# Low parts of two weight halves made in one operation of 4096 columns, with the halves in paired slots

## The reference

```
def swiglu(h, w_gu, w_down):
    g, u = jnp.split(h @ w_gu, 2, axis=-1)
    return (jax.nn.silu(g) * u) @ w_down

def moe_swiglu(h, router_w, w_gu, w_down):
    ...
    for e in range(N_EXPERTS):      # 8 experts, w_gu[e] 1024 x 7168, w_down[e] 3584 x 1024
        out = out + cw[:, e:e + 1] * swiglu(xf, w_gu[e], w_down[e])
```

## Time and profile before

| | |
|---|---|
| median of 3 runs | 1671.43 us (1670.72 to 1672.18) |
| the profiled execution | 1670.79 us |
| its span, first to last instruction | 1669.0 us |
| TensorE busy | 1639.0 us (98%) |
| VectorE busy | 1319.3 us (79%) |
| ScalarE busy | 1102.0 us (66%) |
| read from memory | 484.94 MB, 292 GB/s over the span |

### The profile page before, as it was taken

One profiled execution on the slowest core, in us unless ns is written; L12 is line 12 of the kernel. 1 busy time (PEld: TensorE's weight loads), 2 busy tenths in 40 slices (PEclk: granted clock), 3 DMA queues, 4 the chain that ended last, 5 costly groups with the idle time before them and its releaser, 6 DMA issues.

```text
span 1669.0 us, 23179 instructions
## 1 busy us (share of the span) xinstructions
PE 1639.0 (98%) x8338; PEld 1373.9 (82%) x8338; DVE 1319.3 (79%) x1133; ACT 1102.0 (66%) x1076; POOL 225.6 (14%) x398
## 2 busy tenths in 40 slices
PE   9999999999999999999999999999999999999996
PEld 7988888888889888888888788887888887888875
DVE  6567656545465677468999999889999899998997
ACT  5355744444444557447768887778887688877885
POOL 0034440000000344407920000000000000000000
PEclk9999999999999999999999999999999999999998
DMA  8654544555545444536998999989999899999894
GB/s 339 264 177 152 187 179 164 202 184 193 179 173 177 169 159 171 188 147 254 412 379 348 417 421 401 409 334 397 421 398 418 348 374 419 419 399 379 341 422 199
DMA packets 71792, 488.74 MB, mean 293 GB/s; under 512 B 8651, under 2 KB 11932, under 8 KB 13212
## 3 DMA queue, kind: packets, MB, share of 16 engines
q1 hardware_dynamic: 69052, 483.89, 74.3%
q10 hardware_dynamic: 2656, 3.70, 0.7%
HBM read 484.94 MB, written 2.62 MB: 292 GB/s over the span
## 4 chain that ended last, share of the span: by engine, by line
PE 82%; DVE 9%; DMA 4%; issue 3%; ACT 1%; DVEq 0%; SPq 0%; ACTq 0%
PE bank L418 20%; PE bank L420 20%; PE bank L419 20%; DMA w_raw<-expert_slabs 3%; PE bank L1941 3%; PE bank L1942 3%; DVE w_lo L414 3%; PE bank L1722 3%; PE bank L1724 3%; PE bank L1725 3%; DVE e_v L411 2%; DVE e_uy L414 2%; PE bank L1920 2%; PE bank L1958 1%; DVE e_bias L414 1%
## 5 line engine op out<-in xcount | busy, mean ns | idle before, releaser
L414 DVE TENSOR_TENSOR w_lo<-w_raw,w_hi 128x2048 fp32r<-128x2048 f32 x288 | 654.5, 2292 | 210.2 <-ACT w_hi L405 209.8
L405 ACT ACTIVATE w_hi<-w_raw 128x2048 fp32r<-128x2048 f32 x288 | 551.2, 1918 | 389.3 <-PE bank L420 280.5
L418 PE MATMUL bank<-w_hi,hT 128*128 128x512 f32 x720 | 285.2, 396 | 1.9 <-DVE w_lo L1167 1.9
L420 PE MATMUL bank<-w_hi,hT 128*128 128x512 f32 x720 | 281.3, 391 | 0.0
L419 PE MATMUL bank<-w_lo,hT 128*128 128x512 f32 x720 | 280.8, 390 | 0.0
L418 PEld LDWEIGHTS bank<-w_hi,hT 128*128 128x128 f32 x720 | 135.5, 188 | 28.6 <-issue 2.1
L420 PEld LDWEIGHTS bank<-w_hi,hT 128*128 128x128 f32 x720 | 135.4, 188 | 28.7
L419 PEld LDWEIGHTS bank<-w_lo,hT 128*128 128x128 f32 x720 | 135.7, 188 | 26.8
L414 DVE TENSOR_TENSOR e_uy<-w_raw,e_k 128x2048 fp32r<-128x2048 f32 x56 | 128.2, 2288 | 16.7 <-ACT e_k L405 16.6
L411 DVE TENSOR_TENSOR e_v<-w_raw,hT 128x2048 fp32r<-128x2048 f32 x55 | 125.8, 2288 | 10.8 <-ACT hT L402 10.7
L405 ACT ACTIVATE e_k<-w_raw 128x2048 fp32r<-128x2048 f32 x56 | 107.5, 1920 | 34.3 <-PE bank L420 22.3
(11 more groups left out here) (355 smaller groups left out, 3125.9 us busy)
## 6 DMA issues: line engine op xcount, KB each, us to landing
w_raw<-expert_slabs SPq DMA_DIRECT2D x334, 1024.0 KB, 7.4
w_raw<-mix_slabs SPq DMA_DIRECT2D x88, 1024.0 KB, 4.8
w_raw<-dense_slabs SPq DMA_DIRECT2D x33, 1024.0 KB, 4.8
bias_lines<-bias ACTq DMA_DIRECT2D x1, 1536.0 KB, 7.5
X<-in_x SPq DMA_DIRECT2D x2, 512.0 KB, 5.8
bias<-bias_lines SPq DMA_DIRECT2D x1, 1024.0 KB, 6.8
yT<-in_ffn_norm_g ACTq DMA_DIRECT2D x2, 512.0 KB, 5.0
v_buf<-expert_slabs SPq DMA_DIRECT2D x1, 1024.0 KB, 4.7
```

The source lines that it names most:

```text
L405: act.activation(hi_slot(n), raw_of(n, early), ACT.Copy).then_inc(hi_ready, 1)
L414: eng.tensor_tensor(lo_slot(n), raw_of(n, early), hi_slot(n), ALU.subtract).then_inc(lo_ready, 1)
L418: pe.matmul(dst, hi, whi, start=first, stop=False, skip_group_check=True)
L420: return pe.matmul(dst, lo, whi, start=False, stop=last, skip_group_check=True)
```

## The change

The six raw slots are used so that halves 2d and 2d+1 of an expert block lie side by side, and so do their high and low parts: `e_qv`, `w_split[0:2]`, `w_split[2:4]` for the high ones, `e_bias`, `e_ku`, `w_split[4:6]` for the low ones. The high parts are still cast one by one. The low parts of a pair are made by one VectorE operation of 4096 columns (`split_lo_pair`), which waits for both casts and counts two halves at once. VectorE's lists are rewritten by pairs; ScalarE's and TensorE's lists in the blocks stay. Halves 0 and 1 of block 0 are split in the last steps of the mixer, and the two early loads into other buffers go.

Outside the blocks, three things change. The last two dense steps are written out, with the last turn between the two token tiles of the product before it, and in that norm a low part comes after the first addition of tile 1. The reciprocal root takes one small operation less. At the end, the scatter goes column half by column half into four banks, the squares are summed in four pieces, and one token tile is scaled by ScalarE and sent from its queue.

```
-        w_hi = sb("w_hi", [P, SPLIT, HALF], F32R)
-        w_lo = sb("w_lo", [P, SPLIT, HALF], F32R)
+        w_split = sb("w_split", [P, 2 * SPLIT, HALF], F32R)
+        w_hi, w_lo = w_split[:, 0:SPLIT, :], w_split[:, SPLIT:2 * SPLIT, :]
...
+        moe_hi = (e_qv, w_split[:, 0:2, :], w_split[:, 2:4, :])
+        moe_lo = (e_bias, e_ku, w_split[:, 4:6, :])
...
+        def raw_slot(n):
+            return (n - MOE0 + 2) % RAW if n >= MOE0 else n % RAW
...
-            elif opening and n == MOE0 + 2:
-                job_in_bank(act, DEPTH - 1, ("turn_m", 1), 7)
-            elif opening and n == MOE0 + 3:
-                act.wait_ge(logits_ps, TT)
-            elif opening and n == MOE0 + 4:
-                act.wait_ge(biased, DEPTH * HEADS)
+            elif n < MOE0 + 2 and isinstance(cyc, int) and cyc == 0:
+                job_in_bank(act, DEPTH - 1, ("values", HEADS - 1), 7)
+            elif n < MOE0 + RAW and isinstance(cyc, int) and cyc == 0:
+                act.wait_ge(half_used, MOE0)
...
+        def split_lo_pair(eng, d, cyc=0):
+            def flat(pair):
+                return pair.rearrange("p h c -> p (h c)")
+
+            eng.wait_ge(hi_ready, MOE0 + 2 * d + 2 + RAW * cyc)
+            at = raw_slot(MOE0 + 2 * d)
+            eng.tensor_tensor(flat(moe_lo[d % SPLIT][:, :, :]), flat(w_raw[:, at:at + 2, :]),
+                              flat(moe_hi[d % SPLIT][:, :, :]), ALU.subtract).then_inc(lo_ready, 2)
...
+                    if s == MIX_HALVES - 2 and layer == 1:
+                        split_hi(act, MOE0 + 1)
...
+                    if s == MIX_HALVES - 2 and layer == 1:
+                        dve.wait_ge(half_used, n0 + S_WO)
+                        split_lo_pair(dve, 0)
...
-                norm_lo(q, 0, 1)
+                if q != 2:
+                    norm_lo(q, 0, 1)
                 for hf in range(2):
                     add_sums(q, 1, hf)
                     raw_rows(q, 1, hf)
+                    if q == 2 and hf == 0:
+                        norm_lo(q, 0, 1)
...
-                chain(dve.tensor_scalar(v, v, -0.5, None, ALU.mult))
                 for i in range(3):
                     chain(dve.tensor_tensor(t, y, y, ALU.mult))
-                    chain(dve.tensor_tensor(t, t, v, ALU.mult))
+                    chain(dve.scalar_tensor_tensor(out=t, in0=t, scalar=-0.5, in1=v, op0=ALU.mult, op1=ALU.mult))
...
-                    lo(c, 3, 4)
+                    lo(c, 1)
                     take_y(b)
-                    lo(c, 5, 6, 7, 8, 9)
+                    lo(c, 2, 3, 4)
                     fold_prod(b, i2, 0)
                     for i in range(3):
                         add_scattered(b, i)
                     fold_lo(b, 0, 0)
-                    lo(c, 10)
+                    lo(c, 5)
                     add_scattered(b, 3)
                     if not closing:
                         next_pick(b)
-                    lo(c, 11, 12, 13)
+                    lo(c, 6)
                     fold_prod(b, i2, 1)
-                    lo(c, 14)
+                    lo(c, 7)
                     fold_lo(b, 1, 1)
-                    lo(c, 15, 16, 17, 18, 19)
-                    fold_prod(b, i2, 2)
-                    lo(c, 20)
-                    fold_lo(b, 2, 0)
-                    lo(c, 21, 22, 23, 24)
-                    fold_prod(b, i2, 3)
-                    lo(c, 25)
-                    fold_lo(b, 3, 1)
-                    lo(c, 26, 27, 28, 29, 30)
-                    fold_prod(b, i2, 4)
-                    lo(c, 31)
-                    fold_lo(b, 4, 0)
-                    lo(c, 32, 33, 34, 35, 36)
-                    fold_prod(b, i2, 5)
-                    lo(c, 37)
-                    fold_lo(b, 5, 1)
-                    lo(c, 38, 39)
+                    lo(c, 8, 9)
+                    for m in range(2, MSTEPS - 1):
+                        fold_prod(b, i2, m)
+                        lo(c, 3 * m + 4)
+                        fold_lo(b, m, m % 2)
+                        lo(c, 3 * m + 5)
+                        if m < MSTEPS - 2:
+                            lo(c, 3 * m + 6)
                     fold_prod(b, i2, 6)
-                    lo(c, 40)
                     if closing:
                         fold_lo(b, 6, 0)
-                        lo(c, 41)
                     else:
                         gathered(b + 1, 0)
                         fold_lo(b, 6, 0)
-                        lo(c, 41)
                         gathered(b + 1, 1)
-                        lo(c, 42, 43, 44)
+                        lo(c, 21)
...
                 for i in range(2):
                     gathered(0, i)
+                split_lo_pair(dve, 1)
                 route_gates()
                 make_pick(0, seat_only=True)
-                for i in (2, 3, 4, 5):
-                    split_lo(dve, MOE0 + i)
+                split_lo_pair(dve, 2)
...
+                    down_tile(n, m, 0, ffT_hi, ffT_lo)
+                    if turned:
+                        turn(turned)
+                    down_tile(n, m, 1, ffT_hi, ffT_lo).then_inc(half_used, 1)
...
+                gate_up(n0 + 5, it)
+                down(n0 + 7, it, FSTEPS - 2, turned=FSTEPS - 1)
+                n = n0 + DENSE_HALVES - 1
+                pe.wait_ge(lo_ready, n + 1)
+                down_tile(n, FSTEPS - 1, 0, last_hi, last_lo).then_inc(sum_ps, 1)
+                down_tile(n, FSTEPS - 1, 1, last_hi, last_lo, closing=True).then_inc(half_used, 1)
+                norm_turn(2, 0, 1)
...
+            act.wait_ge(gain_done, 1)
+            act.wait_ge(rs_ready, 5)
+            act.activation(hrow[:, 0, :], hrow[:, 0, :], ACT.Copy, scale=rs[:, 0:1]).then_inc(out_scaled, 1)
+            act.wait_ge(out_scaled, 1)
+            act.dma_start(out[0, 0:P, :], hrow[:, 0, :]).then_inc(out_sent, 16)
...
+            dve.wait_ge(gain_in, 16 * 5)
+            dve.tensor_tensor(hrow[:, 0, :], X[:, 0, :], last_gain[:, :], ALU.mult).then_inc(gain_done, 1)
+            dve.wait_ge(ss_ready, 2 * 4 + 2 * TT)
+            chain(dve.tensor_tensor(ssq[:, :], half_ss[:, 0, :], half_ss[:, 1, :], ALU.add))
             rsqrt_of(ssq[:, :], 1.0 / D)
-            dve.wait_ge(gain_in, 16 * 5)
-            for t in range(TT):
-                dve.scalar_tensor_tensor(out=hrow[:, t, :], in0=X[:, t, :], scalar=rs[:, t:t + 1], in1=last_gain[:, :],
-                                         op0=ALU.mult, op1=ALU.mult).then_inc(hrow_ready, 1)
+            dve.sem_inc(rs_ready, 1)
+            dve.scalar_tensor_tensor(out=hrow[:, 1, :], in0=X[:, 1, :], scalar=rs[:, 1:2], in1=last_gain[:, :],
+                                     op0=ALU.mult, op1=ALU.mult).then_inc(hrow_ready, 1)
...
+                for hf in range(2):
+                    pe.wait_ge(y_lo_ready, 2 * blocks + hf - 1)
+                    for t in range(TT):
+                        cols = slice(CHUNK * hf, CHUNK * (hf + 1))
+                        pe.matmul(bank[2 * hf + t][:, :], spread_r[:, t, :], y_hi[:, cols], start=True, stop=False)
+                        pe.matmul(bank[2 * hf + t][:, :], spread_r[:, t, :], y_lo[:, cols], start=False,
+                                  stop=True).then_inc(scatter_ps, 1)
```

282 lines of the change are left out of this document (130 added, 152 removed).

## The result

The changed kernel takes 1773.8 us (median of 4 runs, 1772.18 to 1778.78) against 1671.7 of the kernel before on the same chip: a ratio of 1.0621, 95% interval 1.0603 to 1.0638. It is 102 us slower. The prediction said slower, 1703; the range ended at 1712. The sign was right and the size was three times too small.

A forecast was written before the change was run, and what follows sets the result against it. TensorE, busy 98%, was taken as the bound, with DMA, ScalarE and VectorE level late in narrow blocks. Terms 27.6 + 7.4 + 1.2 + 1.2 - 3.4 - 2.2 = +31.8 on 1671.4 gave 1703.2 us; 8-in-10 range 1679 to 1712.

The forecast's parts named there:

- The operation: VectorE low parts: one 4096-column operation takes 4.42 us, the next can start after 4.34, saving 0.07 us a pair.
- The direction: Whole kernel: slower, chance 0.84, against faster 0.12 and same 0.04.
- fold_prod behind a whole pair holding ScalarE: Narrow blocks: fold_prod waits for the whole pair, so fold_hi and the next casts wait, 2 us or so three times a block.
- the walk's start: End of block 1: half 31 is cast at 951.0 us, set by the DMA, and no earlier after the change.
- The walk itself: Half 31's cast to block 2's start: 42.3 us, so 993.3 instead of 984.07, +9.2; three times, 27.6.
- Wide blocks: At their entry pair (10,11) comes about 0.4 us late behind the scatter's additions: three times, +1.2.
- Block 7 and the end: Block 7's last product comes 7.4 us later; the end's scatter, additions and multiplies win 2.2.
- Opening: Block 0 after the gather: pair (4,5) is 0.9 us late for TensorE and pair (12,13) adds 0.3, +1.2.
- Dense end and norm: Last dense step's turn waits of 1.5 and 0.6 us and the norm's 1.34 wait for a cast go, -3.4.
- the DMA starves too: Raw slots freed two at a time let half 31 land up to 2.2 us later, four times: 1712; chance 0.10.
- Only latency: Pairs merely wait for their second cast and fold_hi never holds ScalarE up, +2.7 us a narrow block: 1679; chance 0.14.
- faster: No pair waits in narrow blocks; VectorE's savings give 5.9 us and the ends 5.6: 1660; chance 0.12.

The follow-up runs named there:

- its ties put on single operations: Changed kernel with each pair made by two operations; both wait for the second cast, loads wait for both, TensorE waits for both: 1775.2 us.
- the changed order: Changed kernel with every pair's low parts made by two 2048-column operations in the pair's place, VectorE's small operations staying where the change put them: 1693.9 us.
- the old narrow order: Changed kernel with single operations; VectorE's narrow blocks ordered as in the kernel before, wide blocks and opening as changed: 1671.0 us.
- half loads: Changed kernel with pairs, loading only the first 1024 of 2048 columns of each expert half; casts, low parts and products stay: 1736.6 us.
- the single old-order run: Changed kernel with single operations and VectorE's rows in the order of the kernel before; slots, loads and edits at the ends as changed: 1666.1 us.
- the fillers: Changed kernel plus 16 unused 128 x 128 TensorE products before each narrow block's last fold turn and each wide block's first product: 1767.8 us.

## Why the prediction was wrong

- **The operation**: 4.42 us forecast, 4.42 to 4.44 measured; with its ties put on single operations the time is the same. Right.
- **The direction**, and **fold_prod behind a whole pair holding ScalarE**: there in the trace (19.0 us in 8 waits at L936; the forecast had 2 us or so three times a block) and in the runs with single operations (fold_hi waits 8.8 us in the changed order, not at all in the old narrow order, which is 24.5 us faster). Right as a mechanism, but one wait among several: with the pair, fold_prod moved ahead alone gave nothing back.
- **The step that failed is the walk's start: "The DMA sets this ..., and it comes no earlier after the change"**, taken as no later either. Counted from the block's gather, half 31's cast was done at 80.7 us before and at 88.5 after (956.2 less 867.72): 7.8 us late. The pairs had lost this in the part of the block that I did not walk, since I took the landing for given: half 10's cast was 2.9 us late, half 18's 7.1. A pair gives its slots back later (+17.6 us with that tie alone), so the loads start later: half 10's was issued 16.5 us after the gather before and 22.7 after. With half loads half 31's cast is done at 79.8, so this delay is one of supply. The prediction itself named this start as the most likely to break the number.
- **The walk itself** had 42.3 us from there to block 2's start; it took 49.8 (956.2 to 1006.04). Of the 7.5 between, 1.5 arise at pair (38,39), which starts 4.7 us after fold_prod 5 (3.2 in the walk), and 6.0 at pair (40,41), which starts 10.7 after pair (38,39) (4.7 in the walk). Behind both stand the waits of fold_silu on turns 5 and 6, the second with fold_lo 5 behind pair (38,39). I counted fold_prod as moved, but not what TensorE's turns then wait for. The walk's eight hand-overs of 0.05 us rest on no row; they are 0.4 us of it, and in the rows after they run from 0.03 to 0.11. So block 1 lost 9.2 + 7.8 + 7.5 = 24.5 up to block 2's first product: 138.3 us from its gather against 113.8.
- **Wide blocks**: 0.4 each forecast; block 2 lost 3.2 from its first product to its last gather (112.7 against 109.5), 1.8 us of it by the slower clock at its entry (7.2 us for the first 24 products against 5.4). The stretch from gather to gather, forecast as unchanged but for the entry, was 8.5 longer. The three pairs of a narrow and a wide block lost 27.7, 28.5 and 25.4, 81.6 in all, for 28.8 forecast. This one term holds 53 of the 70 us that the sum was short.
- **Block 7 and the end**: +22.6 for +5.2 forecast; it is the same term once more. The edits to the end gave what was said: from fold_lo 6 to the end of VectorE's last multiply it is 17.0 us before and 14.9 in the single old-order run, -2.1 for -2.2.
- **Opening** +2.6 for +1.2. **Dense end and norm** -5.2 up to the first gather for -3.4: the norm's last small operation starts at 478.64 (481.65 before). TensorE is 0.9 us ahead from the first norm on, and only 1.7 are won at the dense end and its norm, half of the term. The other 2.6 come just ahead of the gather and were in no term: in this execution of the kernel before, the granted clock fell to 0.53 in 745 to 755 us, while in the change it was 0.85 in 742 to 750.
- **The rival "the DMA starves too"** named a resource that does starve and mis-sized it: it let half 31 land up to 2.2 us later, once a block; the pairs' delays add up to 7.8 by then. "Only latency" (1679) and "faster" (1660) were further off than the forecast.
- **TensorE's slower clock** stood in no term: 32.4 us more busy time. How much of it could be had back stays open; the fillers, at seven places, took some 17 us of it away and brought 6 to 7.5.

What the Trainium skill says (Perfetto Trace Analysis, Optimizing Scalar/DVE Operations), that larger operations raise throughput if the engine is saturated, and that breaking instructions up may let work end sooner where the engine is not and causes bubbles, is borne out by its second half: VectorE falls from 79% to 74% busy, and breaking the pair up gives 78 us. The first half misled here: in the narrow block 1 VectorE was busy 97 of 103 us before the change. The same page of the Trainium skill (Matmul Optimizations) says that the matmul engine scales its power with its use and wants matmuls back to back in batches. The windows above agree as far as they go: they show the granted clock, 1.00 with the waits filled and 0.76 and 0.85 without, and nothing of the power.

What stays open: why the three ties cost 21 us more together than alone, how the narrow order's 24.5 us are shared between fold_prod and fold_lo, and how the ring in the half-load run shares its 80 us among its links and the order.

## What to carry to other kernels

Before two operations on a chain between engines are made one, count the ties, not the overhead: when the input must be complete, when the buffers go back, when the consumer may start. Where all engines are nearly full in some stage, as in block 1 here (ScalarE busy 85% of it, the others and the DMA 94% and more), walk at least one whole round of the loop that the buffers and in-order queues close, with every wait in both directions, rather than from a point taken as fixed. And a small operation whose place was between the two parts has no good place any more: behind the pair it delays one engine, ahead of it the other.

## What the runs showed of the hardware

TensorE's wait of 3.07 us in the half-load run was followed by eight products some 0.43 us apart and then 0.23 again; after the 3.48 us wait that ended at 1006.04 it was the same, but for the first four products. Such waits cost this kernel time twice: the wait, and a lower granted clock behind it (mean 0.978 over the run against 0.997 with single operations in the old order). With half the bytes a load landed in 4.4 us instead of 7.5, so about 3 of the 7.5 go with the bytes in flight, its own and those of the other loads; the runs do not tell these apart.
